# A second block of the first expert pair's weights in buffers of its own

## The reference, cut to what matters

```python
S, D, E = 256, 1024, 32          # tokens, features, experts
def experts(x, gate, up, down, chosen, weight):
    for e in range(E):
        xe = x[tokens that chose e]
        hid = silu(xe @ gate[e]) * (xe @ up[e])    # 1024 x 512 each in block one, 1024 x 256 in block two
        y[tokens that chose e] += weight * (hid @ down[e])
```

## Time and profile before

| | us |
|---|---|
| median of 3 runs | 2328.48 |
| lowest, highest | 2326.05, 2329.15 |
| the profiled execution | 2326.81 |
| its span from first to last instruction | 2325.1 |

### The profile page before, as it was taken

The page is one execution under the profiler, slowest core; times in us unless marked ns, Lnnn a source line. Parts: engine busy times, 40 slices in busy tenths (PEclk is TensorE's granted clock), DMA queues, the critical chain, the costliest instruction groups (busy, mean ns, idle before and its releaser), DMA issues.

```text
span 2325.1 us, 31808 instructions
## 1 busy us (share of the span) xinstructions
PE 2069.4 (89%) x13718; PEld 1298.9 (56%) x13719; DVE 686.3 (30%) x1451; ACT 421.2 (18%) x814; POOL 0.2 (0%) x4
## 2 busy tenths in 40 slices
PE   7999997677679999876776899999999999999997
PEld 4687643232236774422333568886554778885553
DVE  3884311010007541100100345224211633224113
ACT  2243110000002221100000125202211233103111
POOL 0000000000000000000000000000000000000000
PEclk9999999999999999999999999999999999999999
DMA  9746899999999779999999942257999532468996
GB/s 400 298 193 253 328 418 426 426 426 426 426 425 367 302 318 382 424 426 426 426 426 425 392 154 100 109 223 320 426 424 425 233 143 109 150 258 347 424 424 262
DMA packets 69097, 772.53 MB, mean 332 GB/s; under 512 B 7664, under 2 KB 8176, under 8 KB 10608
## 3 DMA queue, kind: packets, MB, share of 16 engines
q1 hardware_dynamic: 68688, 770.53, 80.3%
q10 hardware_dynamic: 288, 0.26, 0.1%
HBM read 769.72 MB, written 1.05 MB: 331 GB/s over the span
## 4 chain that ended last, share of the span: by engine, by line
PE 60%; DMA 24%; DVE 4%; ACT 1%; issue 1%; SPq 0%; ACTq 0%; DVEq 0%
DMA slab<-in_triples 24%; PE psum L586 16%; PE psum L2390 9%; PE psum L618 9%; PE psum L2422 7%; PE psum L2304 5%; PE psum L931 5%; DVE slab L770 1%; PE psum L2318 1%; PE psum L2351 1%; DMA slab<-in_dense 1%; PE psum L2330 1%; PE psum L2364 1%; PE psum L2358 1%; PE psum L984 0%
## 5 line engine op out<-in xcount | busy, mean ns | idle before, releaser
L2390 PE MATMUL psum<-slab 128*32 128x512 f32 (+1 forms) x3840 | 462.2, 604 | 203.7 <-DMA slab<-in_triples 190.8
L586 PE MATMUL psum<-slab 128*128 128x128 f32 (+4 forms) x2584 | 463.8, 337 | 1.9 <-ACT slab L3238 1.9
L586 PEld LDWEIGHTS psum<-slab 128*128 128x128 f32 (+2 forms) x2584 | 378.3, 189 | 107.4 <-issue 72.9
L2390 PEld LDWEIGHTS psum<-slab 128*32 128x32 f32 x3840 | 149.8, 110 | 511.7 <-DMA slab<-in_triples 285.2
L618 PE MATMUL psum<-slab 128*128 128x256 f32 x1504 | 332.5, 380 | 2.2 <-DVE slab L2600 0.7
L618 PEld LDWEIGHTS psum<-slab 128*128 128x128 f32 x1504 | 283.7, 190 | 49.8 <-issue 5.8
L2422 PE MATMUL psum<-slab 128*32 128x512 f32 (+1 forms) x1920 | 223.0, 596 | 0.6 <-DMA slab<-in_triples 0.6
L2461 DVE TENSOR_TENSOR slab<-psum,slab 128x512 f32<-128x512 f32 (+1 forms) x44 | 24.6, 559 | 626.2 <-PE psum L2390 479.8
L2304 PE MATMUL psum<-slab 128*128 128x256 f32 x704 | 167.9, 380 | 1.2 <-DVE slab L2465 1.2
L2304 PEld LDWEIGHTS psum<-slab 128*128 128x128 f32 x704 | 126.1, 189 | 20.9 <-issue 5.0
L2431 ACT ACTIVATE slab<-psum,slab 128x128 f32<-128x128 f32 x176 | 66.3, 457 | 317.4 <-PE psum L586 317.4
(11 more groups left out here) (441 smaller groups left out, 1363.6 us busy)
## 6 DMA issues: line engine op xcount, KB each, us to landing
slab<-in_triples SPq DMA_DIRECT2D x360, 1536.0 KB, 25.0
slab<-in_dense SPq DMA_DIRECT2D x73, 2048.0 KB, 10.9
slab<-in_pairs SPq DMA_DIRECT2D x14, 2048.0 KB, 8.5
slab<-in_pairs SPq DMA_DIRECT2D x4, 1024.0 KB, 18.2
slab<-in_dense SPq DMA_DIRECT2D x2, 1680.0 KB, 26.0
slab<-in_vec SPq DMA_DIRECT2D x1, 2555.5 KB, 32.8
slab<-in_pairs SPq DMA_DIRECT2D x8, 256.0 KB, 19.7
slab<-in_pairs SPq DMA_DIRECT2D x4, 512.0 KB, 4.4
```

The source lines that it names most:

```text
L586: ins = mm(out_ap, lhs, rhs, start=(n == 0), stop=(n == len(pairs) - 1), skip_group_check=True)
L2390: ins = mm(psum[WIN * g:WIN * g + WIN, n, :], xg[:, k, WIN * g:WIN * g + WIN], weights_of(w, j, g, extra), start=(k == 0), stop=(k == KD - ...
```

## The change

The last block of the pair's projections (kind 1: `pair[3]`, unit 4; kind 2: `pair[1]`, unit 2) was loaded whole into the ring. Now it is split like the last block of all: 3072 of its words go into lent memory (`SPREAD_UP`), 1024 into the ring. So the ring holds 3072 words less of the pair than before, and one more part of the triples fits in it ahead of the phase. To make room, several things move:

- `raw`, the router's working rows, goes to another address.
- `SPREAD_UP` lies in part over `gatedT` and `place`. So `dve_place(q, 0)` moves behind `dve_hidden` of the pair.
- In kind 1 one piece of 512 words lies over constants, so `gla_w2` joins the lent ones. Ahead of the second mixer, 1184 words of constants are loaded again instead of 672, and PE waits for them (`constants_in`) before it uses `gla_w2`.
- In kind 1 the block `pair[4]` (unit 5) now stands in the ring where `pair[3]` (unit 4) stood. In kind 2 the up block's pieces are issued only after `router_ready`.
- PE waits once for both split blocks (`spread_in`, 8 or 7 transfers), at unit 4 in kind 1 and at unit 2 in kind 2.
- The choice of the parts that go to the early buffers shifts by one in kind 2.

```diff
-LENT = ("rw0", "off16", "all64", "cum64", "conv1", "half", "run", "rw1",
+LENT = ("rw0", "off16", "all64", "cum64", "conv1", "gla_w2", "half", "run", "rw1",
...
-LENT_AGAIN = {0: ("half", "rw1"), 1: ("causal", "rw_21"), 2: ("causal", "rw_21")}
+LENT_AGAIN = {0: ("gla_w2", "rw1"), 1: ("causal", "rw_21"), 2: ("causal", "rw_21")}
...
-            n = (6 * i + j + 3) % (NP + len(EARLY_AT))
+            n = (6 * i + j + 2) % (NP + len(EARLY_AT))
...
-        EARLY_FIRST, EARLY_LAST, LATE_LAST = {1: 7, 2: 5}, {1: 4, 2: 5}, {1: 7, 2: 8}
+        EARLY_FIRST, EARLY_LAST, LATE_LAST = {1: 7, 2: 6}, {1: 4, 2: 6}, {1: 8, 2: 9}
         SPREAD = (HO, HO + 512, HO + 1024, HO + 1536, AO + 800 + 17204, VEC + vec_at["rot_a"][0])
+        SPREAD_UP = {1: (AO + 800 + 9728, AO + 800 + 10240, AO + 800 + 10752, AO + 800 + 11264, AO + 800 + 12032, LENT_REST),
+                     2: (AO + 800 + 9216, AO + 800 + 9728, AO + 800 + 10240, AO + 800 + 10752, AO + 800 + 11264, AO + 800 + 12032)}
         HELD = 512 * len(SPREAD)
+        UP_LAST, WHOLE = {1: 3, 2: 1}, {1: (0, 1, 2, 4), 2: (0,)}
+        SPREAD_DMAS = {1: 8, 2: 7}
...
+                    if kind == 1:
+                        sp.dma_start(view(up_at[0], 2048), pair[up, :, 0:2048]).then_inc(sems["spread_in"], 16)
+                        sp.dma_start(view(up_at[4], 512), pair[up, :, 2048:2560]).then_inc(sems["spread_in"], 16)
...
+                def late_fills():
+
+                    sp.wait_ge(sems["router_ready"], 2 * (kind - 1) + l + 1)
+                    if kind == 1:
+                        sp.dma_start(view(up_at[5], 512), pair[up, :, 2560:3072]).then_inc(sems["spread_in"], 16)
+                    else:
+                        sp.dma_start(view(up_at[0], 2560), pair[up, :, 0:2560]).then_inc(sems["spread_in"], 16)
+                        sp.dma_start(view(up_at[5], 512), pair[up, :, 2560:3072]).then_inc(sems["spread_in"], 16)
+                    m = EARLY_FIRST[kind] + LATE
+                    early_fill(m // n, m % n, after_pair)
...
-                for j in range(last):
-                    if ring_fill == EARLY_LAST[kind]:
-                        early_fills()
-                    fill((pair[j], SLOT), at[1] + PAIR_FREE[kind][j])
+                for j in WHOLE[kind]:
+                    fill((pair[j], SLOT), begin + PAIR_FREE[kind][j])
                     ring_fill += 1
-                first = at[0]
-                wait_free(first, SLOT - HELD, at[1] + PAIR_FREE[kind][last])
-                sp.dma_start(view(first, SLOT - HELD), pair[last, :, HELD:]).then_inc(sems["spread_in"], 16)
-                ring_fill += 1
+                if ring_fill == EARLY_LAST[kind]:
+                    early_fills()
+                for j in (up, down):
+                    first = at[0]
+                    wait_free(first, SLOT - HELD, begin + PAIR_FREE[kind][j])
+                    sp.dma_start(view(first, SLOT - HELD), pair[j, :, HELD:]).then_inc(sems["spread_in"], 16)
+                    ring_fill += 1
...
+                    q.e.wait_ge(sems["constants_in"], q.due("constants_in", 16))
                     for h in range(H):
                         ins = mm(banks(6, 2, H, S)[:, h, :], v("gla_w2")[:, P * h:P * h + P], glr, start=True, stop=True)
...
-        raw = view(A0 + 9216, S)
+        raw = view(A0 + 12660, S)
...
         def dve_route2(q, m):
 
             dve_windows(q, m)
-            dve_place(q, 0)
             dve_gathered(q, m)
...
         def dve_pair(q, m, kind):
             dve_hidden(q, kind, 4 if kind == 1 else 2)
+            dve_place(q, 0)
             dve_gathered(q, m)
```

More of the change, by code:

```diff
@@ L428, in experts @@
                 ring_fill, used = 0, [0] * len(EARLY_AT)
-                last = len(PAIR_FREE[kind]) - 1
                 def early_fill(i, j, begin):
@@ L438, in early_fill @@
                     sp.dma_start(view(EARLY_AT[n], PART), triples[i, j]).then_inc(sems[f"early{n}_in"], 16)
+                up, down, up_at = UP_LAST[kind], len(PAIR_FREE[kind]) - 1, SPREAD_UP[kind]
+                begin, n = at[1], TRI_UNITS[kind]
+                after_pair = begin + PAIR_UNITS[kind]
                 def early_fills():
@@ L460, in experts @@
+                at[1] = after_pair
                 for i in range(TRI):
@@ L557, in pass_experts @@
         def pass_experts(q, kind):
-            for _ in range(len(PAIR_FREE[kind]) - 1):
+            for _ in WHOLE[kind]:
                 pass_slot(q)
-            q.at = (q.at + SLOT - HELD) % (NR * SLOT)
+            q.at = (q.at + 2 * (SLOT - HELD)) % (NR * SLOT)
             for i in range(TRI):
@@ L575, in part, with spread_slots @@
             return blocks(parts[:, s, :])
-        def spread_slot(q):
-            first = q.at
-            q.at = (first + SLOT - HELD) % (NR * SLOT)
-            q.e.wait_ge(sems["spread_in"], q.due("spread_in", 64))
-            return [view(at, 512) for at in SPREAD] + [view(first + 512 * j, 512) for j in range((SLOT - HELD) // 512)]
+        def spread_slots(q, kind):
+            own = SLOT - HELD
+            first = (q.at + (SLOT if kind == 1 else 0)) % (NR * SLOT)
+            q.e.wait_ge(sems["spread_in"], q.due("spread_in", 16 * SPREAD_DMAS[kind]))
+            return [[view(at, 512) for at in places] + [view(first + own * n + 512 * j, 512) for j in range(own // 512)]
+                    for n, places in enumerate((SPREAD_UP[kind], SPREAD))]
         def accumulate(out_ap, pairs):
@@ L2311, in pe_pair @@
                     for half in range(2):
-                        w = slot(q)
+                        if n == 1 and half == 1:
+                            up, down = spread_slots(q, kind)
+                            w = None
+                        else:
+                            w = slot(q)
                         if n == 0 and half == 1:
@@ L2318, in pe_pair @@
                                 ins = mm(psum[CAP * e:CAP * e + CAP, n, :], xg[:, k, CAP * e:CAP * e + CAP],
-                                         sl(w, KD)[:, e * (KD // 2) + i, :], start=(k == 0), stop=(k == KD - 1),
-                                         skip_group_check=True)
+                                         up[e * (KD // 2) + i] if w is None else sl(w, KD)[:, e * (KD // 2) + i, :],
+                                         start=(k == 0), stop=(k == KD - 1), skip_group_check=True)
                         ins.then_inc(sems["unit_done"], 1)
@@ L2323, in pe_pair @@
                 for half in range(2):
-                    w = slot(q)
-                    if half == 1:
+                    if half == 0:
+                        w = slot(q)
+                    else:
+                        up, down = spread_slots(q, kind)
                         q.e.wait_ge(sems["xg_ready"], q.due("xg_ready"))
@@ L2337, in pe_pair @@
             q.e.wait_ge(sems["xg_half"], q.due("xg_half"))
-            w = slot(q) if kind == 1 else spread_slot(q)
+            if kind == 1:
+                w = slot(q)
             for half in range(2):
@@ L2342, in pe_pair @@
                     q.e.wait_ge(sems["xg_ready"], q.due("xg_ready"))
-                    if kind == 1:
-                        w = spread_slot(q)
                 for f in range(fc):
```

27 lines of the change are left out of this document (12 added, 15 removed).

## The result

The changed kernel takes 2334.63 us, the median of seven runs (2331.55 to 2337.7), against 2326.96 us (2322.84 to 2329.45) for seven runs of the kernel before beside it. The ratio is 1.0035, with a 95% interval of 1.0025 to 1.0044. The change costs 7.7 us: slower by over 0.2%, while the prediction had +2.5 us and "the same" as the likeliest case. The time itself lies within the predicted range of 2326.5 to 2335.5, close to its upper end, and partly by luck: the range was laid around a median of 2328.48 for the kernel before, and beside the changed kernel that one took 1.5 us less. 7.7 us on top of 2328.48 would be 2336.2, outside the range, and 7.7 is also above the +6.3 that the extremes of the terms gave. The profiled execution took 2335.7 us, its span is 2334.0 us.

The account below looks back on a forecast made before the run. The prediction took the DMA stream to bound the expert phases, its start set by PE finishing the pair. Terms 2.9 - 1.0 + 0.6 gave +2.5 us on the median 2328.48, so 2331.0 us; 8-in-10 range 2326.5 to 2335.5.

Parts of the forecast that it names:

- the extremes of the terms: Whole kernel: all terms at their lower or upper bounds, -0.4 to +6.3 us.
- What bounds the phases: Expert phases: PE waits for the DMA stream, at share 1.00 and 421 to 426 GB/s, idle ahead of each stream.
- The extra part buys nothing in m = 2 and m = 3: Start of these phases: (2,0) waits for unit 4 with or without the preloaded part, so the gain is nothing.
- The late `place`: PE's gather starts 1.24 us later in m = 0, 1.45 in m = 2; +2.9 us for m = 2 and m = 3.
- m = 0 and m = 1: These two phases: the gather's delay less a saving in the 13th part's landing, -1.0 us together, bounds -2.6 to +2.5.
- the saving: m = 0 and m = 1: the 13th part lands 6.9 us after issue instead of 8.5 and 8.7, its queue having emptied.
- The constants: Ahead of the second mixer: 512 more words, 0.26 MB, loaded in a gapless stream, +0.6 us, bounds 0 to 0.6.
- B: Unit 2 in kind 2 waits for the up block's late pieces: slower, 2333.2 us or more; chance 0.18 with upper bounds.
- C: Pair's gather on PE: `place` is hidden and PE starts as before, -2.9 us, 2325.6, no change; chance 0.05.
- A: All four phases: the extra preloaded part pays, 2314 to 2320 us; chance of 2324 or less 0.10.
- The formula: Transfer of one part: about 2.0 us plus its bytes at 436 GB/s, 5.6 us; the prediction used measured 6.1 to 6.9.
- the case "slower": Whole kernel: a measured time slower by more than the 0.2%, 4.7 us, that can be told; chance 0.18.

Follow-up runs that it names:

- e5_place_own: Changed kernel with the first triple's `place` in words of its own, made early in `dve_route2`, `gated` reading it too: 2327.89 us, ratio 1.0001.
- e1_place_back: Changed kernel with the first `place` in its own words, made early in `dve_route2`, `gated` still reading the other `place`: 2327.69 us, ratio 0.9996.
- e6_place_later: Kernel before with `place` behind `dve_hidden` and four more unused VectorE instructions ahead of it: 2345.09 us, ratio 1.0083.
- w1_cut_kind2: Kernel before with part (2,0) of m = 2 and m = 3 cut in two transfers, issued at units 2 and 4: 2325.04 us, ratio 0.9990.
- v2_gather_behind_after: Changed kernel with the first triple's gather moved behind the pair's down projection: 2329.14 us, ratio 1.0007.
- v1: Kernel before with the first triple's gather moved behind the pair's down projection: 2330.2 us, ratio 1.0014.
- e2_place_late: Kernel before with only the first triple's `place` moved behind `dve_hidden`, no memory moved: 2333.49 us, ratio 1.0032.

## Why the prediction was right and wrong

**What bounds the phases: right.** DMA is at 422 and 423 GB/s with a share of 1.00 and 1.01 from the 13th part on, as in the earlier trace rows.

**The extra part buys nothing in m = 2 and m = 3: right, and shown.** With `place` early again these phases are as before within 0.1 us, while the extra part is loaded (`e5_place_own`); in `e1_place_back` they are within 0.2 us, once the 1.6 us of slow clock are taken off. The new idle pieces stand where the prediction put them (291 to 295 was foretold in m = 0; it is 295.3 to 297.4, since the transfers ahead of it ended later, and at some 2 us it is half as long as foretold).

**The late `place`: right in place and size.** Foretold was a wait of 1.24 us in m = 0 and 1.45 us in m = 2. PE's idle time ahead of the gather is 1.13 and 1.35 us, and the 13th part is issued 1.20 us later (62.26 in place of 61.06 us after the first early part) and 1.43 us later (57.09 for 55.66). The end of the phase moved by 1.5 and 1.3 us in m = 2 and m = 3: the +2.9 us of the sum came out as +2.8.

**m = 0 and m = 1: wrong, and this is the whole miss.** The term was -1.0 us for both and came out as +4.4. The step that failed is the saving: "the 13th part follows one part issued 4 us earlier", so it would land 6.9 us after its issue, as the issue at 1607.3 did, in place of 8.5 and 8.7. It took 8.2, 10.1, 9.9 and 8.4 us, a mean of 9.15, while the kernel before has 8.5, 8.7, 9.0 and 7.8, a mean of 8.5. So the saving of 1.6 to 1.8 us is not there. Four landings of each kernel that scatter by 1.2 to 1.9 us don't show that the emptied queue costs anything; with no saving at all, the term is 1.2 us for each phase, and 2.1 and 2.3 were measured. The row that I took the saving from is a single one, of m = 2, with a spacing of 3.4 us. With `place` early the landings are 7.6 and 7.7 us, which is half the saving that I forecast, and the phases gain 1.0 and 0.5 us. The upper bound for this term was +2.5, with no saving; the measured +4.4 lies beyond it.

What stays open is the rest of these two phases. The late `place` alone costs 1.9 and 0.4 us in m = 0 and m = 1, the extra part with an early `place` -1.0 and -0.5; the sum of these is +1.0 and -0.1, not 2.1 and 2.3. Up to the landing of the 20th part the same sum is 2.0 - 0.8 = +1.2 and 1.6 + 0.5 = +2.1 us, against +2.4 and +2.2 measured. So in m = 1 nearly all of the misfit comes from later in the phase, and in m = 0 it stays. Even up to the 20th part the late `place` alone costs more than the 1.2 us of its delay. Behind that I have only the correlation of the last section.

**The constants: right in size.** +0.6 us was foretold, +0.6 measured in two profiles of each kernel. It isn't resolved well: with the constants as before, this stretch took 127.1 to 127.8 us and once 130.0, with the changed ones 127.6 to 128.1 us and once 130.7.

**B, that unit 2 waits for the up block in kind 2: refuted, but with no margin.** The projections of m = 2 run as one piece of 7.09 us. The second piece of the up block was issued at 1595.82 and took 13.4 us, so it was there at 1609.2. PE loads the first weights of unit 2 at 1609.24, and the profile names that transfer as what released them, 0.03 us behind the usual 0.29 between two loads. In m = 3 the piece landed at 2115.1 and the load is at 2115.37, on time. The transfer in m = 2, then the load in m = 2 and in m = 3:

```profile
slab<-in_pairs SPq DMA_DIRECT2D x1, 256.0 KB, 13.4
...
1609.24 0.14 PEld L2357 LDWEIGHTS psum<-slab 128*64 128x64 f32 x2 [0.32 <-DMA slab<-in_pairs]
...
2115.37 0.14 PEld L2357 LDWEIGHTS psum<-slab 128*64 128x64 f32 x2 [0.29 <-DMA slab<-in_pairs]
```

**C, that `place` is hidden: refuted** by the idle times above.

**A: refuted** by `e5_place_own`. The rule that the prediction named for it from the Trainium skill, "DMA: Bandwidth & Descriptors", section "Rules for kernel authors" (issue early, compute, wait late), was followed by the change in all four phases; the runs show 1.5 us for it, all in m = 0 and m = 1. The formula that the prediction took from the same page, section "Anatomy of one DMA", and by which a part takes 5.6 us, is given in the Trainium skill for transfers that GpSimd issues, while these are SP's; measured on an empty queue are 6.0 to 6.6 us for the changed kernel in m = 2 and m = 3.

**The chances.** The movement is +7.7 us, in the case "slower" that had 0.18. The late `place` was foretold; what put the sum too low was above all a saving that was taken from one row. Had I taken no saving, the sum would have been 2.9 + 2.5 + 0.6 = +6.0, slower by over 0.2%.

## What to carry to other kernels

Preloading more pays only if it puts one more transfer ahead of the event from which the stream never idles again; count the transfers up to that event, word by word, and ask which event is next: here it is one unit later and a part shorter, so 2.5 us of earlier transfer bring 0.7 us at best. A buffer that is gained by moving an instruction of 0.43 us can cost more than it brings, since the instruction's delay passes through PE and SP to the stream's start. A transfer that is put behind another wait needs its margin checked at the engine that uses it: here it was nil, and nothing in the total time shows that. Where a forecast takes a saving from a single row, its other end belongs in the sum's weight as well as in the range.

## What the runs showed of the hardware

**Behind idle pieces of 3 us PE's clock fell, behind 1.1 to 1.35 us it didn't.** Behind PE's idle 3.06 and 3.2 us in `e6_place_later` the granted clock was 0.65 and 0.58 of full speed over the next 4 to 5 us, and 3.84 us of gather became 5.46; the same came in all four phases. In the changed kernel the stretches behind 1.13 and 1.35 us of idle time have 1.00:

```profile
287.87:292.00 4.13, 4.13 (x36) 4.03 (x36) 0.26 (x1) 1.51 (x4) 0.00 (x0) 1.00 1.00 425
...
1614.50:1618.00 3.50, 3.42 (x30) 3.42 (x31) 0.03 (x1) 1.32 (x4) 0.00 (x0) 1.00 0.40 164
```

So a wait on PE isn't priced by its length alone. Nor is its length the whole rule. Ahead of the pair in m = 2 and m = 3 PE has two idle pieces, of 0.48 and 0.60 us, in every profile. In three of the 26 phases there (m = 2 of `e1_place_back` and of `w1_cut_kind2`, m = 3 of `v2_gather_behind_after`) the clock fell behind them and everything after came 1.6 us later; in the other 23 it stayed at full speed. The first of the three:

```profile
1592.00:1594.00 2.00, 2.00 (x8) 1.50 (x8) 1.81 (x15) 2.00 (x4) 0.00 (x0) 0.50 0.98 418
1594.00:1596.00 2.00, 2.00 (x5) 0.90 (x4) 1.08 (x6) 1.97 (x5) 0.00 (x0) 0.67 1.04 440
```

0.50 is the level of 1.2 GHz. What made these three differ isn't shown; it is a reason not to read 1 to 2 us from one profile.

**Late landings come with instruction fetches.** In the full stream a part lands 3.69 us after the one before it. In eleven profiles (all but `v1` and `v2`), from the 15th part of a phase on, 64 parts, none to three in a phase, landed 4.2 to 5.3 us after the one before, and each of them has a 16 KB packet of the instruction queue, of about 1 us, within the 5.3 us ahead of its landing; of the 3244 other parts 546 have one as near. The queues in 1.3 us of the changed kernel, 316.0 to 317.3, ahead of a landing at 321.3 that came 5.21 us after the one before (packets, MB, share of 16 engines):

```profile
q1 hardware_dynamic: 46, 0.57, 104.1%
q8 instruction: 1, 0.02, 4.7%
```

4.7% of 16 engines over 1.3 us is one engine for 1 us. No run took the fetches away, so this is a correlation, not a cause that is shown.

**A part that meets an empty queue needs 6.0 to 6.6 us, the one behind it more.** In m = 2 and m = 3 the 13th part, alone on its queue, landed 6.0 to 6.6 us after its issue in the changed kernel. In m = 0 and m = 1, some 4 us behind another one, it took 8.2 to 10.1 us in the changed kernel, 8.2 and 7.7 in `e2_place_late`, and 7.6 and 7.7 in `e5_place_own`.
